# ScalarE waits on its own signals in five places only: one core, a hybrid decoder layer

## The reference

```
cond = silu(c);  shift, scale, gate = split(cond @ w_mod + b_mod)
hn = rmsnorm(x) * (1 + scale) + shift
u  = hn @ w_in                        # 1024 x 8064, split among the branches
ya = rwkv7(...)  * silu(ag)           # state recurrence with a rank-one update
yb = hgrn2(...)  * silu(bg)           # gated linear recurrence, head norm
yc = retention(...) * silu(cg)        # decayed attention in chunks, head norm
yd = rglru(...)  * silu(dg)           # conv, sigmoid gates, scan
merged = sum_b sigmoid(mg_b) * (y_b @ w_branch_b)
out = rmsnorm(x + gate * (merged @ w_out)) * final_g
```

## Time and profile before

| | |
|---|---|
| median of 3 runs | 1146.57 us (1140.64, 1146.57, 1146.66) |
| profiled execution | 1144.64 us, span 1142.8 us |
| TensorE matmul busy | 1069.6 us (94%), 9924 instructions |
| VectorE busy | 588.8 us (52%) |
| ScalarE busy | 327.8 us (29%), 527 instructions |
| GpSimd busy | 376.8 us (33%) |
| mean granted TensorE clock | 0.989 |

### The profile page before, as it was taken

The page is one execution under the profiler, slowest core; times in us unless marked ns, Lnnn a source line. Parts: engine busy times, 40 slices in busy tenths (PEclk is TensorE's granted clock), DMA queues, the critical chain, the costliest instruction groups (busy, mean ns, idle before and its releaser), DMA issues.

```text
span 1142.8 us, 23087 instructions
## 1 busy us (share of the span) xinstructions
PE 1069.6 (94%) x9924; PEld 831.7 (73%) x9924; DVE 588.8 (52%) x1033; ACT 327.8 (29%) x527; POOL 376.8 (33%) x347
## 2 busy tenths in 40 slices
PE   1799998989889999999999999999999989999997
PEld 1677787767667777777777787777777768887885
DVE  5773943785463332333433217647777486423544
ACT  4625213411422122122121134135545341001321
POOL 0342543221356122212222233335333346662000
PEclk9999999999999999999999999999999999999999
DMA  9411111200101011011111121111101026412221
GB/s 377 160 37 37 46 50 52 65 28 24 33 25 39 25 34 39 25 34 39 29 30 34 29 65 37 37 54 38 47 26 49 25 90 208 138 38 93 74 92 55
DMA packets 80101, 70.27 MB, mean 61 GB/s; under 512 B 4096, under 2 KB 72960, under 8 KB 78976
## 3 DMA queue, kind: packets, MB, share of 16 engines
q1 hardware_dynamic: 74528, 49.34, 13.8%
q10 hardware_dynamic: 5472, 19.47, 4.7%
HBM read 64.60 MB, written 4.19 MB: 60 GB/s over the span
## 4 chain that ended last, share of the span: by engine, by line
PE 82%; DVE 11%; ACT 2%; DMA 2%; issue 1%; SPq 0%; POOL 0%; DVEq 0%; ACTq 0%
PE bank L553 53%; PE bank L969 8%; PE bank L599 7%; PE bank L921 1%; DMA slots<-in_w_mod 1%; DVE slots L1886 1%; DVE slots L1726 1%; DVE slots L1477 1%; DVE slots L1530 1%; PE bank L788 1%; PE bank L784 1%; DMA slots<-in_x 1%; DVE stage L1407 1%; PE bank L730 1%; PE bank L700 1%
## 5 line engine op out<-in xcount | busy, mean ns | idle before, releaser
L553 PE MATMUL bank<-hn_hi,w_hi 128*128 128x512 f32 x944 | 389.4, 413 | 7.9 <-ACT slots L1038 3.1
L553 PE MATMUL bank<-hn_lo,w_hi 128*128 128x512 f32 x944 | 369.7, 392 | 0.0
L553 PE MATMUL bank<-hn_hi,w_lo 128*128 128x512 f32 x944 | 369.1, 391 | 0.0
L465 POOL CAST w_hi<-w_raw 128x512 fp32r<-128x512 f32 x118 | 92.1, 780 | 623.6 <-PE bank L553 587.5
L553 PEld LDWEIGHTS bank<-hn_hi,w_hi 128*128 128x128 f32 x944 | 177.7, 188 | 52.8 <-issue 6.8
L553 PEld LDWEIGHTS bank<-hn_hi,w_lo 128*128 128x128 f32 x944 | 177.9, 188 | 39.0
L553 PEld LDWEIGHTS bank<-hn_lo,w_hi 128*128 128x128 f32 x944 | 178.1, 189 | 33.6 <-issue 1.7
L467 POOL TENSOR_TENSOR w_lo<-w_raw,w_hi 128x512 fp32r<-128x512 f32 x118 | 166.1, 1408 | 9.4
L1060 ACT ACTIVATE stage<-bank 128x512 f32<-128x512 f32 x64 | 38.3, 598 | 221.1 <-PE bank L553 194.2
L1038 ACT ACTIVATE slots<-bank 128x512 f32<-128x512 f32 x50 | 30.0, 600 | 156.8 <-PE bank L553 156.5
L1631 DVE TENSOR_TENSOR stage<-stage,bank 128x512 f32<-128x512 f32 x48 | 33.0, 688 | 75.1 <-PE bank L599 74.1
(11 more groups left out here) (308 smaller groups left out, 1452.8 us busy)
## 6 DMA issues: line engine op xcount, KB each, us to landing
w_raw<-in_w_in SPq DMA_DIRECT2D x118, 256.0 KB, 2.9
slots<-in_w_mod SPq DMA_DIRECT2D x8, 1024.0 KB, 8.5
slots<-in_x SPq DMA_DIRECT2D x8, 512.0 KB, 7.7
w_branch<-in_w_branch SPq DMA_DIRECT2D x32, 128.0 KB, 2.7
slots<-in_w_mod ACTq DMA_DIRECT2D x8, 512.0 KB, 4.8
slots<-in_w_out ACTq DMA_DIRECT2D x8, 512.0 KB, 5.7
xr<-in_x ACTq DMA_DIRECT2D x8, 512.0 KB, 3.6
out<-xr ACTq DMA_DIRECT2D x8, 512.0 KB, 2.6
```

The costliest lines, as they stand in the source:

```text
L465: nc.gpsimd.tensor_copy(w_hi[p][:, :, :], w_raw[p][:, :, :]).then_inc(s_w_hi_ready, 1)
L553: last = mm(o, w[p][:, k4, :], h[:, k, n * HALF:(n + 1) * HALF], start=(p == 0 and k4 == 0 and q == 0), stop=(p == 1 and k4 == 3 and q == 2))
```

## The change

Of ScalarE's waits on its own semaphores five remain: behind the squares with a sum (line 994, the sum is read next), behind the evacuation into `b_f_raw` (1036), behind the outputs of retention and HGRN (1136, 1276), and behind the squares of the final norm (1329). Everywhere else `act.wait_ge(s, after(s))` becomes `after(s)`: the semaphore is still raised and still counted, so the other engines' waits keep their numbers. No instruction is added, removed or moved.

```diff
                     nc.scalar.activation(slot(MERGED + i), slot(MERGED + i), ACT.Copy, scale=rs[:, i:i + 1])\
                         .then_inc(s_xn_ready, 1)
-                    act.wait_ge(s_xn_ready, after(s_xn_ready))
+                    after(s_xn_ready)
...
                 nc.scalar.activation(hn_hi[:, k, halves(n)], hn_f32[u % 4], ACT.Copy).then_inc(s_hn_hi_ready, 1)
-                act.wait_ge(s_hn_hi_ready, after(s_hn_hi_ready))
+                after(s_hn_hi_ready)
...
                                                  ACT.Silu if ct in GATED else ACT.Copy).then_inc(s_evac, 1)
-                            act.wait_ge(s_evac, after(s_evac))
+                            after(s_evac)
...
                                          ACT.Copy).then_inc(s_tm_ready, 1)
-                    act.wait_ge(s_tm_ready, after(s_tm_ready))
+                    after(s_tm_ready)
...
                                              bias=pc(bias, j)).then_inc(s_gates_ready, 1)
-                        act.wait_ge(s_gates_ready, after(s_gates_ready))
+                        after(s_gates_ready)
...
                     nc.scalar.activation(slot(12 + j)[:, halves(n)], slot(14 + j)[:, halves(n)], ACT.Square)\
                         .then_inc(s_squares, 1)
-                    act.wait_ge(s_squares, after(s_squares))
+                    after(s_squares)
...
                     nc.scalar.activation(slot(12 + j)[:, halves(n)], bank[4 + 2 * j + n][:, :], ACT.Sqrt,
                                          scale=1.0 / 64, bias=pc("eps")).then_inc(s_roots, 1)
-                    act.wait_ge(s_roots, after(s_roots))
+                    after(s_roots)
...
```

More of the change, by code:

```diff
@@ L985, in _ @@
             nc.scalar.activation(cond, pcs("c"), ACT.Silu).then_inc(s_cond_ready, 1)
-            act.wait_ge(s_cond_ready, after(s_cond_ready))
+            after(s_cond_ready)
             def squares_of_x(n):
@@ L997, in squares_of_x @@
                     .then_inc(s_x_rms, 1)
-                act.wait_ge(s_x_rms, after(s_x_rms))
+                after(s_x_rms)
             def normalise_x(n):
@@ L1084, in _ @@
                 nc.scalar.activation(slot(6 + j), slot(6 + j), ACT.Sqrt, scale=2.0).then_inc(s_lru_mult, 1)
-                act.wait_ge(s_lru_mult, after(s_lru_mult))
+                after(s_lru_mult)
             evac(7)
@@ L1089, in _ @@
             nc.scalar.activation(slot(16)[0:64, :], slot(16)[0:64, :], ACT.Tanh).then_inc(s_a_tanh, 1)
-            act.wait_ge(s_a_tanh, after(s_a_tanh))
+            after(s_a_tanh)
             evac(1)
@@ L1128, in _ @@
                     .then_inc(s_kz_tm_ready, 1)
-                act.wait_ge(s_kz_tm_ready, after(s_kz_tm_ready))
+                after(s_kz_tm_ready)
             evac_turned(CV + 1, 1)
@@ L1163, in decays @@
                     .then_inc(s_a_e_ready, 1)
-                act.wait_ge(s_a_e_ready, after(s_a_e_ready))
+                after(s_a_e_ready)
                 if i:
@@ L1206, in _ @@
                         .then_inc(s_a_y_part, 1)
-                    act.wait_ge(s_a_y_part, after(s_a_y_part))
+                    after(s_a_y_part)
                 merge_gate()
@@ L1214, in _ @@
                 nc.scalar.activation(b_f[j], b_f_raw[j], ACT.Sigmoid).then_inc(s_b_f_sig, 1)
-                act.wait_ge(s_b_f_sig, after(s_b_f_sig))
+                after(s_b_f_sig)
             act.wait_ge(s_merged, 32)
@@ L1220, in _ @@
                 nc.scalar.activation(b_f[j], b_f[j], ACT.Ln).then_inc(s_b_lnf, 1)
-                act.wait_ge(s_b_lnf, after(s_b_lnf))
+                after(s_b_lnf)
             evac(2)
@@ L1229, in _ @@
             nc.scalar.activation(dz[0][:, :, :, :], dz[0][:, :, :, :], ACT.Exp).then_inc(s_b_e_ready, 1)
-            act.wait_ge(s_b_e_ready, after(s_b_e_ready))
+            after(s_b_e_ready)
             evac(1)
@@ L1238, in _ @@
                 nc.scalar.activation(slot(12 + j), b_f_raw[j], ACT.Sigmoid, scale=-1.0).then_inc(s_b_k_sig, 1)
-                act.wait_ge(s_b_k_sig, after(s_b_k_sig))
+                after(s_b_k_sig)
             evac(2)
@@ L1258, in _ @@
                         .then_inc(s_b_p_ready, 1)
-                    act.wait_ge(s_b_p_ready, after(s_b_p_ready))
+                    after(s_b_p_ready)
                     for nb in (0, 2):
@@ L1315, in split_merged @@
                     .then_inc(s_merged_hi_ready, 1)
-                act.wait_ge(s_merged_hi_ready, after(s_merged_hi_ready))
+                after(s_merged_hi_ready)
             act.wait_ge(s_merged, 64)
@@ L1331, in _ @@
                     .then_inc(s_h_rms, 1)
-                act.wait_ge(s_h_rms, after(s_h_rms))
+                after(s_h_rms)
                 act.wait_ge(s_out_ready, tt + 1)
```

24 lines of the change are left out of this document (12 added, 12 removed).

## The result

The changed kernel takes 1140.74 us (median of 10 runs) against 1146.62 us (10 runs) of the kernel before. The ratio is 0.9948, with a 95% interval of 0.9929 to 0.9968. That is 5.9 us less, against a forecast of 1141.6 us (5.0 us under the median that I had) and a range of 1136.5 to 1146.5 us. With 0.52% it lies just beyond what I called measurable. One of the ten runs took 2622.77 us; it is in that median and not in the ratio, and the other nine have a median of 1140.18 us. The profiled execution took 1140.06 us, 4.6 us less than the profiled one of before.

What follows compares the result with a forecast made beforehand. TensorE, busy 94% of the span, was taken as the bound, so only its stalls behind ScalarE could gain. Terms summed to 3.99, say 4.0 us, giving 1141.6 us, midway between 1140.6 (profiled run) and 1142.6 (median); range 1136.5 to 1146.5 us.

Steps and rivals of the forecast that it cites:

- Start: 36.7 to 42.1 us, four in-place normalisations and the first cast of line 1014: closer spacing gains 0.60 us.
- Gates of the LRU: 99 to 107 us: earlier load and closer sigmoids 0.5 us, root and two evacuations 0.30 us, together 0.8 us.
- Second gates: 195 to 204 us: the evacuation before the casts of line 1093 loses its wait, gaining 0.15 us.
- Roots: 216 to 219 us: load 0.24 us earlier and second root closer, starting VectorE's long chain earlier; 0.39 us.
- The pairs at 251 and 295 us: Two evacuations at 251.03 us and two at 295.09 us, TensorE waiting behind each pair; 0.30 us in all.
- Turned tiles of B: Four evacuations of branch B from 721.45 us, after which TensorE resumes from a 1.80 us stall; 0.45 us.
- HGRN's norm: 913.9 to 919.6 us: squares shrink, the load runs earlier, the root starts 1.30 us earlier, and all of it passes.
- a rival, tied to the stall at 939 us: Faster: the 6.8 us half-clock stretch behind that stall vanishes, 3.1 us more, 7.1 in all, 1138.5 us; chance 0.24.
- a load that needs a dry pipeline: Rival: hoisted table loads wait for a drained pipeline, so three gain nothing and line 1118 loses 1.04 us; 1144.7 us, chance 0.03.
- no overlap: Rival: in-place or PSUM-reading activations don't overlap with neighbours, only gaps and loads count, 2.2 us; 1143.4 us, chance 0.13.
- slower clock: Rival: three stalls at 127.9, 294.6 and 722.2 us each get a half-clock stretch costing 1.7 us; 1146.7 us, chance 0.07.
- nothing on the path: Rival: each TensorE stall ends for another reason than the profile row says; 1145.6 us, chance 0.03.

Runs made afterwards that it cites:

- before_warm: The kernel before, all waits kept, with four unread float32 matmuls filling TensorE's stall at 939 us; 1145.94 us, ratio 0.9996.
- norm_only: The kernel before without the own waits of the squares and roots of HGRN's norm alone; 1144.86 us, ratio 0.9983.
- all_but_norm: The changed kernel with the two own waits of HGRN's norm put back; 1140.33 us, ratio 0.9948 to the kernel before.
- loads_only: The kernel before without the own wait directly ahead of the table loads of lines 1073, 1118 and 1287 only; 1144.04 us, ratio 0.9976.
- late_only: The kernel before with only the own waits behind the roots of line 1118 removed; 1147.2 us, ratio 0.9997.

## Why the prediction was right, and where it was off

The forecast of 1141.6 us came true to 0.9 us, and its mechanism is the one that the stages show: pairs 0.14 to 0.15 us closer, three loads that run in ScalarE's idle time, and shorter stalls of TensorE where it waited for them. The size came out right partly by luck, for a reason that I had given to a rival. Term by term (stages of the changed kernel against before):

- **Start**: 0.56 us, forecast 0.60. Every kernel with this part of the change has it.
- **Gates of the LRU**: 0.73 us from TensorE's first gate (99.04 us before, 99.43 after) to its return (129.20 and 128.86), forecast 0.80. Of it VectorE's second multiply comes 0.38 us earlier, forecast 0.5: the load at line 1073 has lost its 0.25 us, but the sigmoids soon wait for TensorE (the last start of the group has 0.17 us of idle time in front), which I forecast. The root and the two evacuations give the other 0.35 us, forecast 0.30.
- **Second gates**: 0.21 us, forecast 0.15. The five kernels without the early waits have both terms, to 0.02 us.
- **Roots**: forecast 0.39 us, nothing arrives. The load of line 1118 starts earlier by its 0.25 us against what is ahead of it, and VectorE's chain gives it back:

```profile
226.04 1.23 DVE L1532 SCALAR_TENSOR_TENSOR slots<-slots 128x1024 f32<-128x1024 f32 x1
```

```profile
224.88 1.30 POOL L467 TENSOR_TENSOR w_lo<-w_raw,w_hi 128x512 fp32r<-128x512 f32 x1
```

```profile
224.38 1.29 POOL L467 TENSOR_TENSOR w_lo<-w_raw,w_hi 128x512 fp32r<-128x512 f32 x1
...
225.10 1.65 DVE L1532 SCALAR_TENSOR_TENSOR slots<-slots 128x1024 f32<-128x1024 f32 x1
```

  The first two fences are the timeline of before, the third that of the changed kernel. Line 1532 takes 0.42 us more where it starts while more of GpSimd's TENSOR_TENSOR is still to run. In all 14 profiles it ends 1.08 to 1.11 us after that TENSOR_TENSOR (before, 227.27 against 226.18 us; after, 226.75 against 225.66), whether it starts 0.14 or 0.57 us before GpSimd's end. So an earlier root could buy nothing there: the chain's next step came when GpSimd's split of the weights was done, and that had moved with TensorE only (its line 553 releases GpSimd's line 465 just ahead, in both). The prediction had no term for GpSimd.
- **The pairs at 251 and 295 us**: 0 and 0.14 us, forecast 0.15 each.
- **Turned tiles of B**: 0.47 us, forecast 0.45.
- **HGRN's norm**: 1.28 us, forecast 1.30. Load and squares work as written: the load alone 0.95 us, the squares alone nothing, both 1.28 to 1.34 us.
- **The tail and the RWKV chunks**: nothing, as forecast.

The sum of the stages is 0.56 + 0.73 + 0.21 + 0.14 + 0.47 + 1.28 = 3.4 us instead of 4.0. The terms that were mis-sized are the roots (0.39 us, where GpSimd was left out) and the pair at 251 us (0.15 us); the others are off by 0.07 us or less.

The other 2.5 us of the 5.9 us between the medians are not shown by any stage. The stretches at half clock are of the right size. From the counts above, (5/6 − 1/5) times about 3 us, and 3/6 times 2.7 us, make some 3 us, an estimate from eleven profiles of different kernels on several chips. I had this only as a rival, tied to the stall at 939 us. That stall's stretch can go (1.8 us), but the kernels in which it goes or halves, before_warm and norm_only, don't get faster by more than their intervals. The dear stretches were at 200 and 250 us, and the profile before me didn't show them, since it was one of the lucky executions. The footing midway between profile and median hid this as scatter: I wrote that the runs lie 6.0 us apart and didn't ask what made them so. So a forecast of 4.0 us from a footing 1.0 us under the median met 3.4 us of stages and some 2.5 us of something else.

Rivals that fell: a load that needs a dry pipeline (all three start 0.01 to 0.02 us behind an activation), no overlap (0.14 to 0.15 us a pair), slower clock in the form that I gave it (no stretch appeared behind the stalls at 128, 295 or 722 us in any profile), nothing on the path. The Trainium skill, "ScalarE: Activation LUTs", section "What ACT_TABLE_LOAD costs", puts a DRAIN of about 1.38 us beside each load. The trace doesn't show one: of the changed kernel's 51 loads of 1.28 us, the 33 for which the trace shows no wait start 0.02 us (17 to 19 ns) behind the activation ahead of them.

## What to carry to other kernels

An own wait that is removed is worth its idle time only where another engine stands still behind it. The 14 waits in the chunk loops made no difference that could be measured, since TensorE had filler work there. The waits around one table load took 1.3 us off their stage, 0.95 us of it by the one directly ahead of the load. And where VectorE's next step ended with GpSimd's in every profile, an earlier root bought nothing. Ask of each such load which wait it carries, because the gain is ScalarE's idle time ahead of it. Where runs of one kernel scatter by 1%, profile the same kernel twice before crediting an edit: here two executions of the same instructions differed by 7 us, mostly through the length of half-clock stretches. That is more than the edit's own 3.4 us, and useless matmuls in TensorE's stalls won 0.35% without one wait removed.

## What was not expected of the hardware

- Stretches at 1.2 GHz of 3.4, 6.8 or 10.2 us stood behind stalls of TensorE of 2.65 to 4.04 us, of different length from execution to execution, and sometimes absent (none behind 3.40 us in all_but_norm, none behind 2.86 us in loads_only). The longest cost 3 us each. The stalls of 1.3 to 1.8 us at 128, 295 and 722 us had none, but one of 1.63 us at 836 us had one in late_only.
- A VectorE SCALAR_TENSOR_TENSOR of 128x1024 took up to 1.65 instead of 1.23 us beside GpSimd's TENSOR_TENSOR, and ended 1.08 to 1.11 us after it in all 14 profiles.
- An ACT_TABLE_LOAD starts 0.01 to 0.02 us after an activation that is not waited for, and the next activation as soon after the load.
